# Two output tiles of a weight chunk take turns, matmul by matmul

## The chip, the cores and the metric

The kernel runs on one core of a Trainium2 chip. The metric is the device time of one execution in microseconds; smaller is better. Times before are three runs; the profile is of one execution.

## What is computed

A transformer-like stack on a sequence of 512 tokens with a model width of 1024, all in float32: twice (feed-forward, a mixer of three attention-like branches, feed-forward), then a second mixer and a feed-forward, then a last norm. Most of the arithmetic is products of an activation (1024 or 2816 by 512, held transposed) with a weight matrix. Cut to what matters:

```python
def swiglu_ffn(x, norm, w_gate, w_up, w_down):
    h = rms_norm(x, norm)
    return (jax.nn.silu(h @ w_gate) * (h @ w_up)) @ w_down

    for l in range(DEPTH):
        x = x + 0.5 * swiglu_ffn(x, ffn1_norm[l], ffn1_w_gate[l], ffn1_w_up[l], ffn1_w_down[l])
        h = rms_norm(x, mix_norm[l])
        aq, ak, av, bq, bk, bv, cq, ck, cv, cg, gates = jnp.split(h @ w_in[l], split_points, axis=-1)
...
        x = x + merged.astype(x.dtype) @ w_out[l]
        x = x + 0.5 * swiglu_ffn(x, ffn2_norm[l], ffn2_w_gate[l], ffn2_w_up[l], ffn2_w_down[l])
```

## The kernel before

Every product with a weight matrix goes through `linear` (or, where the output is wanted with tokens on the partitions, through `linear_tok`, which the change does not touch). The float32 operands are split into a high and a low part: a weight chunk `k_raw` becomes `k_wh` (ScalarE copies it, rounded) and `k_wl` (VectorE subtracts), an activation tile `k_x` becomes a high tile (`k_xh`, `k_uh`, the even tiles of `k_G`) and a low one (`k_xl`, `k_ul`, the odd ones). A product is then three matmuls into one PSUM bank: high weight by high activation, high weight by low activation, low weight by high activation. In the profile these are the rows `bank<-k_xh,k_wh`, `bank<-k_xl,k_wh` and `bank<-k_xh,k_wl`.

`linear` walks over its output columns in groups of 256, which are two output tiles (`nt` is 2) with a PSUM bank each. The four banks of `self.LIN` (bank0 to bank3) serve it, so one pair is drained while the next is filled. For a group it walks over the rows of the weights in chunks of up to four tiles of 128 (`kc`), 512 KB each. Within a chunk, before, the loop over the two tiles `m` is outside and the loop over the up to four `k` inside: 12 matmuls into one bank, then 12 into the other. There are 12,168 such matmuls (12,144 of them in pairs of tiles); `linear_tok` has 672 more.

At the first chunks and at each chunk's start, `chunk` emits a weight split two chunks ahead, into one of three buffers (`SPLIT`), which takes its place in ScalarE's and VectorE's queues behind what is already there. Each queue is played strictly in the order in which this Python program appended to it.

Other work is written as generators in `self.bg` (norms, attention, drains of finished banks). `quantum` lets every generator take one step. What a step appends to PE's queue stands between two matmuls of the linear; I call such a piece a burst. Some generators hold a step back until the program's own estimate of PE's clock has passed the estimated end of what they wait for (`ready`). Before, `quantum` is called after every third matmul of a linear.

When a group is finished, its two drains are appended to `self.bg`, each with the token `done[m]` of the last matmul into its bank. The first matmul into a bank waits for the drain that freed it (`fr`).

Two places matter below. In the first feed-forward, the first groups use `k_uh` and `k_ul`, which are the input times its gain but not yet divided by its root mean square; the drains `dgate` and `dup` multiply by it (`self.R`, `k_r`) afterwards. It comes out of `norm_r`: a matmul `bank<-k_acc,k_const` over the summed squares, three ScalarE steps, three VectorE steps. And at the end of a mixer, `merged` (`k_m0mrg`) is split into `k_xh` and `k_xl` before the `w_out` linear can begin.

Of the kernel before, what the change touches and what calls it, by code (L numbers as in the profile page):

```python
# [11 lines left out]
P = 128  # L12
# [112 lines left out]
class Program:  # L125
# [228 lines left out]
    def linear(self, name, l, r0, kts, c0, ncols, act, drain, rate=1, kc=KC):  # L354

        t = 0
        for g in range(0, ncols, 256):
            nt = min(256, ncols - g) // P
            banks = [self.take(self.LIN) for _ in range(nt)]
            done = [None] * nt  # L360
            k0 = 0
            while k0 < kts:
                kt = min(kc if nt == 2 else 2 * kc, kts - k0)
                i, wh, wl, th, tl = self.chunk(name, l, r0 + k0 * P, kt, c0 + g, nt * P)
                for m in range(nt):
                    b, fr = banks[m]
                    for k in range(kt):
                        xh, xl, t1, t2 = act(k0 + k)
                        lh, ll = wh[:, k, m * P:(m + 1) * P], wl[:, k, m * P:(m + 1) * P]
                        first, end = k0 + k == 0, k0 + k == kts - 1  # L370
                        self.mm(fr + [th, t1], b, lh, xh, first, False)
                        self.mm([t2], b, lh, xl, False, False)
                        last = k == kt - 1
                        tok = self.mm([tl], b, ll, xh, False, end, inc=last)
                        if not last:
                            self.quantum(rate)
                    done[m] = tok
                    if m < nt - 1:
                        self.quantum(rate)
                self.release(i, done[-1])  # L380
                k0 += kt
                if k0 < kts:
                    self.quantum(rate)
            for m in range(nt):
                self.bg.append(drain(t + m, banks[m][0], done[m]))
            t += nt
            self.quantum(rate)
# [1264 lines left out]
```

How the kernel before makes its waits and increments, by code:

```python
    def play(self, eng):  # L102
        for kind, a, b in self.items:
            if kind == 0:
                eng.wait_ge(a, b)
            elif kind == 1:
                a(eng)
            else:
                a(eng).then_inc(b, 1)
# [117 lines left out]
    def load(self, out, src, w=()):  # L227
        self.nld += 1
        self.G.wait(w)
        sem = self.ldsem
        self.G.run(lambda e: e.dma_start(out, src).then_inc(sem, 16))
# [1 line left out]
    def load_t(self, i, out, src, w):  # L234
        self.ntl[i] += 1
        self.G.wait(w)
        sem = self.tsem[i]
        self.G.run(lambda e: e.dma_start(out, src).then_inc(sem, 16))
        return (f"t{i}", sem, 16 * self.ntl[i])
# [29 lines left out]
    def _dma(self, i):  # L270
        name, l, r0, kt, c0, n = self.plan[i]
        w = self.d[name]
        src = w[l, r0:r0 + kt * P, c0:c0 + n].rearrange("(k p) n -> p k n", p=P)
        dst = self.RW[i % RAW][:, 0:kt * n].rearrange("p (k n) -> p k n", k=kt)
        self.S.wait(self.raws.pop(i - RAW, []))
        sem = self.rawsem[i % RAW]
        self.S.run(lambda e: e.dma_start(dst, src).then_inc(sem, 16))
# [762 lines left out]
    def mixer2(self, nextg):  # L1040
# [26 lines left out]
                    src = self.d[nm][0, 2 * m + j]  # L1067
                    sem = self.wbsem
                    self.G.run(lambda e, dst=dst, src=src, sem=sem: e.dma_start(dst, src).then_inc(sem, 16))
        twb = ("wb", self.wbsem, 16 * 16)
```

## Time and profile before

| | us |
|---|---|
| median of 3 runs | 3420.56 |
| lowest, highest | 3419.51, 3420.67 |
| span of the profiled execution | 3420.8 |

The profile gives no other time for its own execution than its span, which is 0.2 us above the median of the three runs and 0.1 us above the slowest of them. PE is TensorE's matmuls, PEld its weight loads, DVE is VectorE, ACT is ScalarE. A matmul's row shows its start and a length of about 0.39 us, but the next one starts about 0.23 us later: they overlap. So distances between starts are what counts.

### The profile page before, as it was taken

Reading aid. Unit: us, or ns where it says so; the run is one execution under the profiler, and the core shown is the slowest. Engines: PE = TensorE matmul, PEld = TensorE weight load, DVE = VectorE, ACT = ScalarE, POOL = GpSimd, SP = SyncE. Lnnn points to the kernel's source line nnn. Section 1 sums busy time; section 2 is a strip of 40 time slices with the busy share of each in tenths; the row PEclk is TensorE's granted clock in tenths of the full one; section 3 lists DMA queues with packets and bytes.
Section 4 is the critical chain, followed back from the end, with each engine's and each line's share of the span. In section 5 each row is a group of like instructions: output and inputs, shape, how many; then the busy total and the mean of one; then the engine's idle time right before and its main releaser. Section 6 shows DMA issues by size and latency. Waiting matters only on the chain.

```text
span 3420.8 us, 35895 instructions
## 1 busy us (share of the span) xinstructions
PE 3363.2 (98%) x14282; PEld 2601.9 (76%) x14282; DVE 1746.2 (51%) x2858; ACT 1255.8 (37%) x1891; POOL 28.6 (1%) x57
## 2 busy tenths in 40 slices
PE   7999999999999999999999999999999998999998
PEld 6888866577788888888876666888888756878886
DVE  6333687635463335433487744455334557884333
ACT  4222446424243233322355533334223346343232
POOL 0000000000000000000000000000000100000000
PEclk9999999999999999999999999999999999999999
DMA  4333321222223332333321222323332533323332
GB/s 140 102 95 90 94 73 53 71 80 77 93 87 105 93 95 90 105 99 95 96 85 51 71 64 78 92 92 94 99 93 87 109 61 50 84 80 99 98 91 70
DMA packets 282071, 297.66 MB, mean 87 GB/s; under 512 B 9776, under 2 KB 270256, under 8 KB 281904
## 3 DMA queue, kind: packets, MB, share of 16 engines
q1 hardware_dynamic: 277408, 283.15, 28.9%
q0 software_dynamic: 3536, 10.55, 1.0%
q8 instruction: 112, 1.84, 0.2%
q10 hardware_dynamic: 960, 1.67, 0.1%
q14 instruction: 55, 0.45, 0.0%
HBM read 293.24 MB, written 2.10 MB: 86 GB/s over the span
## 4 chain that ended last, share of the span: by engine, by line
PE 91%; DVE 5%; ACT 2%; issue 1%; DMA 0%; DVEq 0%; SPq 0%; ACTq 0%
PE bank L218 90%; ACT k_sc L214 1%; PE bank L224 1%; DVE k_wl L170 1%; DVE k_sc L180 1%; DVE k_sc L196 0%; DMA k_raw<-in_ffn_w_gate 0%; ACT L208 0%; DVE k_sc L170 0%; DVE k_x L180 0%; ACT k_wh L214 0%; DVE k_xc L180 0%; DVE k_xl L170 0%; DVE k_cv L180 0%; DVE k_ul L170 0%
## 5 line engine op out<-in xcount | busy, mean ns | idle before, releaser
L170 DVE TENSOR_TENSOR k_wl<-k_raw,k_wh 128x1024 fp32r<-128x1024 f32 x545 | 654.6, 1204 | 1178.6 <-ACT k_wh L214 1178.4
L218 PE MATMUL bank<-k_xh,k_wh 128*128 128x512 f32 x2376 | 960.7, 404 | 5.0 <-ACT k_wh L214 3.3
L218 PE MATMUL bank<-k_xh,k_wl 128*128 128x512 f32 x2376 | 928.9, 391 | 4.7 <-DVE k_wl L170 4.7
L218 PE MATMUL bank<-k_xl,k_wh 128*128 128x512 f32 x2376 | 928.4, 391 | 1.7 <-DVE k_xl L170 1.7
L214 ACT ACTIVATE k_wh<-k_raw 128x1024 fp32r<-128x1024 f32 x545 | 563.9, 1039 | 990.3 <-PE bank L218 721.6
L218 PEld LDWEIGHTS bank<-k_xh,k_wh 128*128 128x128 f32 x2376 | 447.2, 188 | 164.1 <-issue 67.9
L218 PEld LDWEIGHTS bank<-k_xh,k_wl 128*128 128x128 f32 x2376 | 447.5, 188 | 100.3 <-DVE k_wl L170 5.5
L218 PEld LDWEIGHTS bank<-k_xl,k_wh 128*128 128x128 f32 x2376 | 447.8, 188 | 96.7 <-issue 8.1
L218 PE MATMUL bank<-k_uh,k_wh 128*128 128x512 f32 x512 | 206.2, 403 | 18.6 <-ACT k_uh L214 18.5
L218 PE MATMUL bank<-k_Ga,k_wh 128*128 128x512 f32 x704 | 218.2, 391 | 0.0
L218 PE MATMUL bank<-k_Gb,k_wh 128*128 128x512 f32 x704 | 218.2, 391 | 0.0
L218 PE MATMUL bank<-k_uh,k_wl 128*128 128x512 f32 x512 | 202.5, 396 | 3.8 <-DVE k_wl L170 3.8
L218 PE MATMUL bank<-k_ul,k_wh 128*128 128x512 f32 x512 | 201.7, 394 | 0.2 <-DVE k_ul L170 0.2
L214 ACT ACTIVATE k_sc<-bank 128x512 f32<-128x512 f32 x160 | 94.6, 596 | 243.8 <-PE bank L218 243.8
L218 PEld LDWEIGHTS bank<-k_Ga,k_wh 128*128 128x128 f32 x704 | 132.2, 188 | 28.0
L218 PEld LDWEIGHTS bank<-k_Gb,k_wh 128*128 128x128 f32 x704 | 132.2, 188 | 28.0
L218 PE MATMUL bank<-k_Ga,k_wl 128*128 128x512 f32 x352 | 138.0, 392 | 0.0
L218 PE MATMUL bank<-k_Gb,k_wl 128*128 128x512 f32 x352 | 138.0, 392 | 0.0
L218 PEld LDWEIGHTS bank<-k_uh,k_wh 128*128 128x128 f32 x512 | 96.8, 189 | 42.4 <-ACT k_uh L214 19.0
L218 PEld LDWEIGHTS bank<-k_ul,k_wh 128*128 128x128 f32 x512 | 97.0, 189 | 25.5 <-issue 2.9
L218 PEld LDWEIGHTS bank<-k_uh,k_wl 128*128 128x128 f32 x512 | 97.0, 189 | 24.8 <-DVE k_wl L170 4.5
L213 ACT ACTIVATE k_sc<-k_sc,k_sm 128x128 f32<-128x128 f32 (+3 forms) x160 | 88.8, 555 | 70.9 <-DVE k_sm L175 70.8
(278 smaller groups left out, 3687.9 us busy)
## 6 DMA issues: line engine op xcount, KB each, us to landing
k_raw<-in_w_in SPq DMA_DIRECT2D x153, 512.0 KB, 3.7
k_raw<-in_ffn_w_gate SPq DMA_DIRECT2D x88, 512.0 KB, 3.8
k_raw<-in_ffn_w_up SPq DMA_DIRECT2D x88, 512.0 KB, 3.8
k_raw<-in_ffn_w_down SPq DMA_DIRECT2D x80, 512.0 KB, 3.4
k_raw<-in_w_out SPq DMA_DIRECT2D x28, 512.0 KB, 3.4
k_raw<-in_w_gate SPq DMA_DIRECT2D x22, 512.0 KB, 3.8
k_raw<-in_w_up SPq DMA_DIRECT2D x22, 512.0 KB, 3.8
k_raw<-in_w_down SPq DMA_DIRECT2D x20, 512.0 KB, 3.4
```

Source lines behind the costliest of these rows:

```text
L170: return q.op(lambda e: e.tensor_tensor(out, a, b, op), cost(out))
L180: return self.V.op(lambda e: e.scalar_tensor_tensor(out=out, in0=a, scalar=s, in1=b, op0=op0, op1=op1), cost(out))
L213: return self.A.op(lambda e: e.activation(out, a, f, bias=bias, scale=scale, accum_out=accum), c + 0.1)
L214: return self.A.op(lambda e: e.activation(out, a, f, bias=bias, scale=scale), c)
L218: fn = lambda e: e.matmul(out, l, r, start=start, stop=stop, skip_group_check=True)
L224: fn = lambda e: e.transpose(out, a, ident)
```

## The change

The loop over `k` is now outside, and inside it the two tiles take turns at each of the three products: high by high for tile 0 and tile 1, high by low for both, low by high for both. The sums into each bank are the same ones in the same order.

```diff
@@ -362,21 +362,19 @@
                 i, wh, wl, th, tl = self.chunk(name, l, r0 + k0 * P, kt, c0 + g, nt * P)
-                for m in range(nt):
-                    b, fr = banks[m]
-                    for k in range(kt):
-                        xh, xl, t1, t2 = act(k0 + k)
-                        lh, ll = wh[:, k, m * P:(m + 1) * P], wl[:, k, m * P:(m + 1) * P]
-                        first, end = k0 + k == 0, k0 + k == kts - 1
-                        self.mm(fr + [th, t1], b, lh, xh, first, False)
-                        self.mm([t2], b, lh, xl, False, False)
-                        last = k == kt - 1
-                        tok = self.mm([tl], b, ll, xh, False, end, inc=last)
-                        if not last:
+                for k in range(kt):
+                    xh, xl, t1, t2 = act(k0 + k)
+                    first, end, last = k0 + k == 0, k0 + k == kts - 1, k == kt - 1
+                    cols = [slice(m * P, (m + 1) * P) for m in range(nt)]
+                    for m in range(nt):
+                        b, fr = banks[m]
+                        self.mm(fr + [th, t1], b, wh[:, k, cols[m]], xh, first, False)
+                    for m in range(nt):
+                        self.mm([t2], banks[m][0], wh[:, k, cols[m]], xl, False, False)
+                    for m in range(nt):
+                        done[m] = self.mm([tl], banks[m][0], wl[:, k, cols[m]], xh, False, end, inc=last)
+                        if not last or m < nt - 1:
                             self.quantum(rate)
-                    done[m] = tok
-                    if m < nt - 1:
-                        self.quantum(rate)
                 self.release(i, done[-1])
```

Three places of the built programs show it. In each row, the tile left of the arrow is written and those right of it are read; trailing numbers are buffer numbers.

**The first chunk, PE.** Before, here from the tenth matmul of the kernel, the twelfth is the last into bank0 and the thirteenth the first into bank1:

```order
L218 MATMUL bank0<-k_uh_124,k_wh_113 128x512
L218 MATMUL bank0<-k_ul_125,k_wh_113 128x512
L218 MATMUL bank0<-k_uh_124,k_wl_114 128x512
L218 MATMUL bank1<-k_uh_124,k_wh_113 128x512
L218 MATMUL bank1<-k_ul_125,k_wh_113 128x512
L218 MATMUL bank1<-k_uh_124,k_wl_114 128x512
```

Now, from the first matmul of the kernel:

```order
L218 MATMUL bank0<-k_uh_124,k_wh_113 128x512
L218 MATMUL bank1<-k_uh_124,k_wh_113 128x512
L218 MATMUL bank0<-k_ul_125,k_wh_113 128x512
L218 MATMUL bank1<-k_ul_125,k_wh_113 128x512
L218 MATMUL bank0<-k_uh_124,k_wl_114 128x512
L218 MATMUL bank1<-k_uh_124,k_wl_114 128x512
```

Neighbours write different banks and read the same activation tile; the calls of `quantum` stand behind the fifth and sixth of six matmuls in place of behind the third and sixth.

**The first norm, PE.** The matmul over the summed squares (`k_acc_120`) of the first feed-forward stands behind 66 matmuls of linears before; the rows end at the 69th:

```order
L218 MATMUL bank3<-k_uh_124,k_wh_113 128x512
L218 MATMUL bank3<-k_ul_125,k_wh_113 128x512
L218 MATMUL bank3<-k_uh_124,k_wl_114 128x512
L218 MATMUL bank4<-k_acc_120,k_const_115 128x512
L218 MATMUL bank3<-k_uh_124,k_wh_113 128x512
L218 MATMUL bank3<-k_ul_125,k_wh_113 128x512
L218 MATMUL bank3<-k_uh_124,k_wl_114 128x512
```

Now it stands behind 71, one before the last of the third chunk (the rows end at the 73rd):

```order
L218 MATMUL bank3<-k_uh_124,k_wh_113 128x512
L218 MATMUL bank2<-k_ul_125,k_wh_113 128x512
L218 MATMUL bank3<-k_ul_125,k_wh_113 128x512
L218 MATMUL bank2<-k_uh_124,k_wl_114 128x512
L218 MATMUL bank4<-k_acc_120,k_const_115 128x512
L218 MATMUL bank3<-k_uh_124,k_wl_114 128x512
L218 MATMUL bank2<-k_uh_124,k_wh_113 128x512
```

It has moved by five matmuls, from the middle of the third chunk to its end, where the next weight split is emitted.

**The same norm, ACT and DVE.** ACT, from the table load ahead of it; before, `k_sc<-bank,k_eps` and the two `k_r` are the norm's steps, and the next weight split (`k_wh`) comes four rows behind them, outside this piece:

```order
L214 ACTIVATE k_wh<-k_raw 128x1024
L214 ACTIVATE k_sc<-bank,k_eps 128x512
L214 ACTIVATE k_r<-k_sc 128x512
L214 ACTIVATE k_r<-k_r 128x512
L214 ACTIVATE k_xh<-k_sc 128x512
L214 ACT_TABLE_LOAD
```

Now:

```order
L214 ACTIVATE k_wh<-k_raw 128x1024
L214 ACTIVATE k_sc<-bank,k_eps 128x512
L214 ACTIVATE k_r<-k_sc 128x512
L214 ACTIVATE k_r<-k_r 128x512
L214 ACTIVATE k_wh<-k_raw 128x1024
L214 ACTIVATE k_xh<-k_sc 128x512
L214 ACT_TABLE_LOAD
```

A `k_wh` stands directly behind the norm's two `k_r`. DVE, before: the norm's three steps are the second to fourth row, and the `x2` row behind `k_x` is the two drains of the first group:

```order
L170 TENSOR_TENSOR k_wl<-k_raw,k_wh 128x1024
L180 SCALAR_TENSOR_TENSOR k_sc<-k_sc,k_r 128x512
L170 TENSOR_TENSOR k_sc<-k_sc,k_r 128x512
L180 SCALAR_TENSOR_TENSOR k_r<-k_sc,k_r 128x512
L180 SCALAR_TENSOR_TENSOR k_sc<-k_x,k_vec,k_r 128x512
L170 TENSOR_TENSOR k_sc<-bank,k_r 128x512 x2
L170 TENSOR_TENSOR k_wl<-k_raw,k_wh 128x1024
```

Now:

```order
L170 TENSOR_TENSOR k_wl<-k_raw,k_wh 128x1024 x2
L180 SCALAR_TENSOR_TENSOR k_sc<-k_sc,k_r 128x512
L170 TENSOR_TENSOR k_sc<-k_sc,k_r 128x512
L180 SCALAR_TENSOR_TENSOR k_r<-k_sc,k_r 128x512
L180 SCALAR_TENSOR_TENSOR k_sc<-k_x,k_vec,k_r 128x512
L170 TENSOR_TENSOR k_sc<-bank,k_r 128x512 x2
L170 TENSOR_TENSOR k_sc<-bank,k_sc 128x512
```

The second weight split (`x2` in the first row) stands ahead of the norm's three steps; before, it stood behind the two drains.

## Rows read from the trace of the kernel before

**Rows 1.** The page, whole span: busy time by engine; the chain that ended last.

```profile
PE 3363.2 (98%) x14282; PEld 2601.9 (76%) x14282; DVE 1746.2 (51%) x2858; ACT 1255.8 (37%) x1891; POOL 28.6 (1%) x57
...
PE bank L218 90%; ACT k_sc L214 1%; PE bank L224 1%; DVE k_wl L170 1%; DVE k_sc L180 1%; DVE k_sc L196 0%; DMA k_raw<-in_ffn_w_gate 0%; ACT L208 0%; DVE k_sc L170 0%; DVE k_x L180 0%; ACT k_wh L214 0%; DVE k_xc L180 0%; DVE k_xl L170 0%; DV
```

**Rows 2.** Timeline, PE, first stage (start us, length us, what).

```profile
22.82 0.39 PE L218 MATMUL bank<-k_uh,k_wl 128*128 128x512 f32 x1
23.05 0.39 PE L218 MATMUL bank<-k_uh,k_wh 128*128 128x512 f32 x1
23.28 0.39 PE L218 MATMUL bank<-k_ul,k_wh 128*128 128x512 f32 x1
```

**Rows 3.** Timeline, PE, in `linear_tok`: two ends of 30 matmuls.

```profile
745.80 0.39 PE L218 MATMUL bank<-k_wh,k_xh 128*128 128x512 f32 x1
...
752.38 0.39 PE L218 MATMUL bank<-k_wl,k_xh 128*128 128x512 f32 x1
```

**Rows 4.** Timeline, PE, `linear` at 1000 us: two ends of 52 matmuls.

```profile
1000.15 0.39 PE L218 MATMUL bank<-k_ul,k_wh 128*128 128x512 f32 x1
...
1011.82 0.39 PE L218 MATMUL bank<-k_ul,k_wh 128*128 128x512 f32 x1
```

**Rows 5.** Timeline, PE, an attention matmul and the two behind it.

```profile
468.64 0.49 PE L218 MATMUL bank<-k_m0qkva 64*128 64x128 f32 x2
469.05 0.50 PE L218 MATMUL bank<-k_wh,k_xh 128*128 128x512 f32 x1
469.39 0.40 PE L218 MATMUL bank<-k_wh,k_xl 128*128 128x512 f32 x1
```

**Rows 6.** Timeline, 35 to 44 us, PE, ACT and DVE.

```profile
35.41 1.02 PE L218 MATMUL bank<-k_acc,k_const 128*128 128x512 f32 x2
...
43.15 0.39 PE L218 MATMUL bank<-k_uh,k_wh 128*128 128x512 f32 x1
...
36.86 0.67 ACT L214 ACTIVATE k_sc<-bank,k_eps 128x512 f32<-128x512 f32 x1
...
38.23 0.63 ACT L214 ACTIVATE k_r<-k_r 128x512 f32<-128x512 f32 x1
...
37.52 1.23 DVE L170 TENSOR_TENSOR k_wl<-k_raw,k_wh 128x1024 fp32r<-128x1024 f32 x1 [1.13 <-ACT k_wh L214]
38.89 0.69 DVE L180 SCALAR_TENSOR_TENSOR k_sc<-k_sc,k_r 128x512 f32<-128x512 f32 x1 [0.15 <-ACT k_r L214]
...
41.07 0.75 DVE L180 SCALAR_TENSOR_TENSOR k_sc<-k_x,k_vec,k_r 128x512 f32<-128x512 f32 x1
41.74 1.28 DVE L170 TENSOR_TENSOR k_sc<-bank,k_r 128x512 f32<-128x512 f32 x2
```

**Rows 7.** Timeline, start of the first `w_out`, PE and DVE.

```profile
936.40 0.40 PE L218 MATMUL bank<-k_m0yc,k_wl 128*128 128x512 f32 x1
937.60 0.47 PE L218 MATMUL bank<-k_xh,k_wh 128*128 128x512 f32 x1 [0.81 <-ACT k_xh L214]
938.90 0.50 PE L218 MATMUL bank<-k_xl,k_wh 128*128 128x512 f32 x1 [0.82 <-DVE k_xl L170]
...
936.83 0.69 DVE L180 SCALAR_TENSOR_TENSOR k_sc<-k_sc,bank 128x512 f32<-128x512 f32 x1 [1.29 <-PE bank L218]
...
938.16 2.49 DVE L170 TENSOR_TENSOR k_xl<-k_m0mrg,k_xh 128x512 fp32r<-128x512 f32 x4
```

**Rows 8.** Stretches (us, busy (x count) of PE, PEld, DVE, ACT, POOL, PEclk, DMA, GB/s).

```profile
940.00:944.00 4.00, 4.00 (x12) 3.16 (x11) 4.00 (x7) 2.05 (x4) 0.00 (x0) 0.57 0.00 0
944.00:948.00 4.00, 4.00 (x19) 3.30 (x18) 0.90 (x2) 1.06 (x1) 0.00 (x0) 1.00 0.39 131
```

**Rows 9.** Waits of PE: us in total, times, longest.

```profile
PE bank L218 <- DVE k_wl L170: 8.5, 3, 4.1
...
PE bank L218 <- DVE k_pt L188: 2.8, 1, 2.8
```

**Rows 10.** Timeline, DVE, the last linear's drains.

```profile
3400.99 0.69 DVE L180 SCALAR_TENSOR_TENSOR k_x<-bank,k_x 128x512 f32<-128x512 f32 x1 [8.04 <-PE bank L218]
```

## The prediction

> **What bounds the kernel now.** I read the page first. PE is busy for 98% of the span and the chain that ended last runs through `bank L218` for 90% [rows 1]: the reader is to see that nothing but the pace of the matmuls, and the places where PE waits, can move the time. The loads are as many as the matmuls (14,282 each) and are covered. Then the timeline of PE gives the pace. In `linear`, 51 distances between starts take 11.67 us, 0.229 us each [rows 4]. The list of PE's waits names only few and short ones in the middle [rows 9]. So the 12,168 matmuls of `linear` at 0.229 are some 2,786 us of the 3420.8.
>
> **The bank change.** Now neighbours write different banks all along. The kernel before has such neighbours at times, so their price can be read off. The twelfth matmul of the kernel (22.82) is the last into bank0, the next (23.05) the first into bank1: 0.23 us, and the one behind it, in the same bank as its forerunner, again comes after 0.23 [rows 2]. In `linear_tok` the bank changes after every sixth matmul, twice as often as in `linear`, and 29 distances with four or five changes among them take 6.58 us, 0.227 each [rows 3]; 51 distances of `linear` with four or five changes have 0.229 [rows 4]. More changes do not go with a slower pace, so a change costs nothing. Nor do rows 2 show a gain at one. With some 11,100 changes added (12,144 less about 1,000 that were there), I price the change of bank at 0. Two distances rounded to 0.01 leave room for 0.01 either way; a cost of that size is excluded by `linear_tok`, a gain is the rival that is far from the rest, and stands there with its chance.
>
> The Trainium skill (TensorE: Matmul & The Clock Gate, "Back-to-back issue gap") gives for 512 columns an isolated gap of about 216 ns. This trace shows 229. Were the difference of 13 ns due to the bank and given back, it would be some 158 us, about 3262.
>
> As a mechanism of this kernel it would be a PSUM bank that is still being written when the next matmul wants it; the rival further down prices that from rows.
>
> Two more things of the new order cost nothing by rows: that neighbours read the same moving tile (in `linear_tok` the first and second of three do, at 0.227, [rows 3]), and that weights now alternate (there is a load to each matmul already, [rows 1]).
>
> **What the change moves.** Five places, each worked out with 0.229 a matmul.
>
> First, the first group's drains, in the first feed-forward. The norm's matmul moves back by five, 1.14 us, from 35.41 to 36.55; it takes 1.02, so ScalarE begins about 37.7. Its three steps took from 36.86 to 38.86, 2.0 us [rows 6], so they end at 39.7. Before, VectorE then began the norm's last steps at 38.89 and the first drain of the banks at 41.74, 2.85 later [rows 6]. Now a weight split stands between: 1.04 on ScalarE and about 1.2 on VectorE (the row at 37.52 has 1.23). That puts the norm's steps at 41.9, the first drain at 44.75, its end (0.64, half of 1.28) at 45.4, the second one's at 46.0. PE wants bank0 at 43.15 [rows 6]; before, the drain was done 0.8 earlier. So it stands 2.25 us, and since its second matmul now wants bank1 at once and not twelve matmuls later, another 0.4: **2.65**. If ScalarE's first step comes as late behind the matmul as before (1.45) it is 3.0; if the split's two steps overlap others, 1.5. Behind the waiting matmul stands all of PE's queue, so the whole of it counts.
>
> Second, the clock. After PE had been idle for two stretches of 0.8 us close to each other at 937 to 939 us [rows 7], the granted clock was 0.57 over 940 to 944, 12 matmuls in place of 4.00 / 0.229 = 17.5, and 1.00 behind it [rows 8]: 5.5 x 0.229 = **1.3**, the level of 1.2 GHz for most of that stretch. A stall of 2.65 is at least as long. Either 0 or 1.3; I take 1.3.
>
> Third, the two starts of `w_out`. `merged` is needed whole. Before, tile 0 of the last pair was done 12 matmuls ahead of tile 1, and VectorE had worked it off; it took up tile 1 at 936.83 and the low splits at 938.16 [rows 7]. Now both are done within one matmul, VectorE begins at 936.6 and has four steps of 0.69 in place of two, so the splits begin at 939.3, 1.15 later. The low product is now the third matmul and not the second, which covers 0.23. PE loses 0.9 each time, twice: **1.8**. Both ends: 0, if the split were still covered, and 2 x 1.4 = 2.8, four steps less two without any cover.
>
> Fourth, the end. The last chunk has two `k`, so tile 0 led by six matmuls and VectorE's drain began at 3400.99 [rows 10], with a strictly serial chain behind it up to the output. It leads by one now: 5 x 0.229 = **1.1** later. Nothing covers it.
>
> Fifth, the gain. The low weights are wanted by the fifth matmul of a chunk in place of the third. PE waited for them three times, 8.5 us in all [rows 9], and each wait becomes 2 x 0.229 shorter: **-1.4**.
>
> Everything else that the later `done[0]` delays (drains of other groups) is read by nobody for a whole group of 24 or 48 matmuls, 5.5 or 11 us, against 1.4 us of drains; I cost it at nothing. If that cover went, PE would wait at most those 1.4 us at a group.
>
> **The bursts.** Steps of the background work now come two close together and then none for five matmuls. Counted in the built programs, 202 bursts with a matmul of 64 rows or columns stay 202, and all bursts go from 315 to 307. A burst with such a matmul has an exit price: from 468.64 over 469.05 to 469.39 are 0.75 us for 128 columns in four passes (0.21) and one matmul (0.23), so 0.3 more [rows 5]. Their number stays, so 0. New is that 81 matmuls stand alone between two bursts, which occurs nowhere before. The nearest row is the distance behind a burst, 0.34 in place of 0.23 [rows 5]: a lone matmul might pay it once more or be spared it, 81 x 0.11 = 9 us either way. I take 0, because the switches between the two kinds of matmul are the same in number.
>
> In the second mixer the bursts move by up to 77 matmuls, so PE's wait of 2.8 us for `k_pt` [rows 9] can go, or another come; 0, between -2.8 and +2.8.
>
> **Sum.** 2.65 + 1.3 + 1.8 + 1.1 - 1.4 = 5.45. On the profiled execution's 3420.8 that is 3426.25; its span is 0.2 above the median, so I predict 3426, 0.16% slower than 3420.56. What a measurement of this kernel can tell from no change is about 0.2%, 6.8 us (3427.4). I forecast no difference that can be told, on the slow side.
>
> **The rivals.**
> - *Slower: the lone matmuls.* If each of the 81 pays the 0.11 again, 9 us come on top: 3435. For it: nothing in the trace shows that one matmul is enough to get back the overlap. Against it: the number of switches is the same. It decides from 0.02 us each on, with the sum above. 0.20.
> - *The first stall does not come* (the split is done earlier than the queue suggests, or the planner's distance suffices): 2.65 + 1.3 go, 3422. Against it: the queues are strictly in order, and the drains had 0.8 us left before. 0.10, of which 0.03 with a lucky second mixer and spared bursts below 3413.7.
> - *Faster: the bank was a limit after all.* 12,144 x (0.229 - 0.213) = 194 us, 3226. For it: 512 columns at 2.4 GHz, one a cycle, would be 0.213. Against it: rows 2 to 4. 0.04.
> - *Slower by the clock.* The Trainium skill (same page, "A second HAM failure mode: psum-queue depth-cycling") tells of a kernel that cycled through banks and idled so briefly and often that the clock kept falling. As a mechanism here: every bank change would have to leave a gap, and the clock fall as in rows 8; then a tenth of the linears at half pace would be 12,168 x 0.1 x 0.2 = 243 us, 3664. Against it: bank changes leave no gap in rows 2 and 4. 0.02.
> - My forecast has the rest, 0.64, and its own range is 3419 to 3432. Its terms can add up to more than 6.8 us (stall 3.0, `w_out` 2.8, second mixer +2.8), so I count 0.16 of it as slower.
>
> **How the numbers follow.** Faster: 0.04 + 0.03 = 0.07. Slower: 0.16 + 0.20 + 0.02 = 0.38. Same: 0.48 + 0.07 = 0.55. The range leaves out the two far cases (0.06) and something at each side: below, the unknown costs of the second mixer and of spared bursts, above, the lone matmuls with the forecast's upper terms. 3418 to 3438.
>
> **What would show it.** In the profile after: PE's distances in a long run of `linear` still 0.229 (right) or nearer 0.215 (the bank was a limit). A wait of PE of 2 to 3 us for VectorE's `k_sc` around 43 us, with a stretch of granted clock near 0.5 behind it. The low product of both `w_out` about 1 us later behind the end of the branch. The last chain about 1 us longer. PE's waits for `k_wl` three, some 7 us. Behind lone matmuls between bursts, a distance of 0.34 or more twice would show the first rival. The prediction is wrong if PE's pace changes at all: 0.001 us a matmul is 12 us.

## The result, and the profile after

The changed kernel takes 3436.81 us (median of 4 runs, 3433.58 to 3438.15), against 3420.61 of the kernel before in the same session (4 runs, 3419.51 to 3421.85): a ratio of 1.0046, 95% interval 1.0034 to 1.0058. It is slower by 0.5%, over twice the 0.2% (6.8 us) that the prediction gave as the least that can be told from no change. The prediction was 3426, within a range of 3418 to 3438, with most of its chance on no difference that can be told.

The profiled execution is the fastest of the four: 3433.58 us, span 3431.8. In the runs listed the time is 1.8 to 2.0 us above the span. So the profiled execution of the kernel before (span 3420.8) was one of some 3422.7 us, about 2 us above its median, and not 0.2 as the prediction had it. The two traces are therefore 11.0 us apart and the medians 16.2. What the traces can explain is the 11.0.

The page after, the lines that answer to [rows 1]:

```profile
PE 3361.6 (98%) x14282; PEld 2606.0 (76%) x14282; DVE 1738.0 (51%) x2853; ACT 1253.3 (37%) x1898; POOL 28.6 (1%) x57
...
PE bank L218 91%; PE bank L224 1%; ACT k_sc L214 1%; DVE k_wl L170 1%; DVE k_sc L180 1%; DVE k_sc L196 0%; DMA k_raw<-in_ffn_w_gate 0%; DVE k_sc L170 0%; ACT k_wh L214 0%; ACT L208 0%; DVE k_x L180 0%; DVE k_xc L180 0%; DVE k_cv L180 0%; DV
```

PE is as busy as before, to 1.6 us. The pace has not changed either. PE in `linear` at 1000 us, where each row is now two matmuls into two banks; the two ends of 27 rows:

```profile
1004.24 0.62 PE L218 MATMUL bank<-k_uh,k_wl 128*128 128x512 f32 x2
...
1016.14 0.62 PE L218 MATMUL bank<-k_ul,k_wh 128*128 128x512 f32 x2
```

From the first to the last are 26 rows, 52 distances, in 11.90 us: 0.229 each, as in [rows 4], now with a change of bank at every one.

From the waits of PE over the whole kernel, those at the end and at the two starts of `w_out` (us in total, times, longest):

```profile
PE bank L218 <- DVE k_acc L170: 3.9, 1, 3.9
...
PE bank L218 <- DVE k_xl L170: 3.4, 2, 1.7
```

And the start of the kernel, which answers to [rows 6]: PE, then ACT, then DVE.

```profile
36.53 1.02 PE L218 MATMUL bank<-k_acc,k_const 128*128 128x512 f32 x2
...
45.41 0.50 PE L218 MATMUL bank<-k_uh,k_wh 128*128 128x512 f32 x1 [2.13 <-DVE k_sc L170]
...
38.98 0.63 ACT L214 ACTIVATE k_r<-k_r 128x512 f32<-128x512 f32 x1
39.51 1.04 ACT L214 ACTIVATE k_wh<-k_raw 128x1024 fp32r<-128x1024 f32 x1
...
40.69 1.23 DVE L170 TENSOR_TENSOR k_wl<-k_raw,k_wh 128x1024 fp32r<-128x1024 f32 x1 [1.97 <-ACT k_wh L214]
41.83 0.68 DVE L180 SCALAR_TENSOR_TENSOR k_sc<-k_sc,k_r 128x512 f32<-128x512 f32 x1
...
44.67 1.28 DVE L170 TENSOR_TENSOR k_sc<-bank,k_r 128x512 f32<-128x512 f32 x2
```

The norm's matmul stands at 36.53, the split `k_wh` directly behind the norm's two `k_r`, the norm's steps on VectorE begin at 41.83 (before: 38.89), the drain at 44.67 and PE goes on at 45.41, after 2.13 us of idling. The prediction had these at 36.55, 41.9, 44.75 and 45.4.

Where the time comes in shows when the same matmul is looked up in both traces. The n-th matmul of the linears (`linear` and `linear_tok` together, 12,840) starts at:

| n | before | after | later by |
|---|---|---|---|
| 66 | 35.19 | 35.16 | 0.0 |
| 97 | 43.15 | 45.41 | 2.3 |
| 240 | 75.88 | 80.20 | 4.3 |
| 3312 (last ahead of the first `w_out`) | 936.40 | 940.49 | 4.1 |
| 8592 | 2308.61 | 2312.57 | 4.0 |
| 10176 (second mixer begins) | 2670.25 | 2674.21 | 4.0 |
| 10608 | 2833.85 | 2830.41 | -3.4 |
| 10800 | 2890.89 | 2897.34 | 6.4 |
| 11350 (its end) | 3062.71 | 3073.53 | 10.8 |
| 12840 (last) | 3401.94 | 3412.76 | 10.8 |

Three stretches matter: 4.3 us in the first feed-forward, 6.9 in the second mixer, and 1.1 at the end, of which the trace shows 0.2 (below). Between 80 and 2670 us little is left on balance (0.4 us gained), although bursts with lone matmuls between them lie all along it.

The waits of PE in the second mixer grow by the same 6.9. Of the kernel before, beside the 8.5 for `k_wl` and the 2.8 for `k_pt` in [rows 9], which all lie here:

```profile
...
PE bank L218 <- ACT k_wh L214: 3.3, 1, 3.3
...
PE bank L218 <- ACT k_ycat L214: 0.8, 2, 0.6
PE bank L224 <- DVE k_xdt L170: 0.8, 1, 0.8
PE bank L218 <- DVE k_ycat L170: 0.4, 2, 0.2
PE bank L218 <- DVE k_sc L170: 0.4, 1, 0.4
PE bank L218 <- DVE k_xc L180: 0.4, 1, 0.4
PE bank L218 <- DVE k_ul L170: 0.2, 1, 0.2
```

And of the changed one, all of them:

```profile
PE bank L218 <- ACT k_wh L214: 11.9, 2, 9.4
PE bank L218 <- DVE k_wl L170: 3.6, 2, 3.5
PE bank L224 <- DVE k_xdt L170: 3.3, 1, 3.3
PE bank L224 <- DVE k_sc L175: 2.2, 1, 2.2
PE bank L218 <- DVE k_x L180: 1.4, 1, 1.4
PE bank L224 <- DVE k_pt L188: 1.1, 1, 1.1
PE bank L218 <- DVE k_x L170: 0.6, 1, 0.6
PE bank L218 <- DVE k_sc L170: 0.4, 1, 0.4
```

They add up to 17.6 us before and 24.5 after. It is not one wait that grew: `k_wl` went from 8.5 to 3.6, `k_wh` from 3.3 to 11.9, and `k_xdt`, `k_sc` and `k_x` are new or longer.

### The profile page after: what moved, and what is told of

The parts are those of the page before. It is cut to its first block, busy times and chain, and to the rows that moved or that the text cites. A ratio compares the mean times of both kernels' runs of the same rounds, so it can differ in the third digit from the quotient of the medians.

```text
span 3431.8 us, 35884 instructions
## 1 busy us (share of the span) xinstructions
PE 3361.6 (98%) x14282; PEld 2606.0 (76%) x14282; DVE 1738.0 (51%) x2853; ACT 1253.3 (37%) x1898; POOL 28.6 (1%) x57
## 4 chain that ended last, share of the span: by engine, by line
PE 92%; DVE 4%; ACT 2%; issue 1%; DMA 0%; DVEq 0%; SPq 0%; ACTq 0%
PE bank L218 91%; PE bank L224 1%; ACT k_sc L214 1%; DVE k_wl L170 1%; DVE k_sc L180 1%; DVE k_sc L196 0%; DMA k_raw<-in_ffn_w_gate 0%; DVE k_sc L170 0%; ACT k_wh L214 0%; ACT L208 0%; DVE k_x L180 0%; DVE k_xc L180 0%; DVE k_cv L180 0%; DVE k_xc L170 0%; ACT k_ycat L214 0%
## 5 line engine op out<-in xcount | busy, mean ns | idle before, releaser
L218 PE MATMUL bank<-k_xh,k_wl 128*128 128x512 f32 x2376 | 774.7, 399 | 0.2 <-DVE k_wl L170 0.2
L218 PE MATMUL bank<-k_xh,k_wh 128*128 128x512 f32 x2376 | 746.7, 395 | 13.5 <-ACT k_wh L214 11.9
L218 PE MATMUL bank<-k_xl,k_wh 128*128 128x512 f32 x2376 | 735.9, 391 | 3.4 <-DVE k_xl L170 3.4
L218 PE MATMUL bank<-k_Gb,k_wh 128*128 128x512 f32 x704 | 190.3, 392 | 0.0
L218 PE MATMUL bank<-k_Ga,k_wh 128*128 128x512 f32 x704 | 190.3, 392 | 0.0
L218 PE MATMUL bank<-k_uh,k_wh 128*128 128x512 f32 x512 | 164.2, 401 | 22.2 <-ACT k_uh L214 18.5
L218 PE MATMUL bank<-k_uh,k_wl 128*128 128x512 f32 x512 | 164.0, 400 | 3.5 <-DVE k_wl L170 3.5
L218 PE MATMUL bank<-k_ul,k_wh 128*128 128x512 f32 x512 | 160.3, 395 | 0.0
L170 DVE TENSOR_TENSOR k_sc<-bank,k_sc 128x512 f32<-128x512 f32 x110 | 75.6, 687 | 130.2 <-PE bank L218 128.7
L180 DVE SCALAR_TENSOR_TENSOR k_x<-bank,k_x 128x512 f32<-128x512 f32 x104 | 69.7, 686 | 87.1 <-PE bank L218 86.3
```

Of the source, the lines that this page charges most:

```text
L170: return q.op(lambda e: e.tensor_tensor(out, a, b, op), cost(out))
L180: return self.V.op(lambda e: e.scalar_tensor_tensor(out=out, in0=a, scalar=s, in1=b, op0=op0, op1=op1), cost(out))
L218: fn = lambda e: e.matmul(out, l, r, start=start, stop=stop, skip_group_check=True)
```

## The experiments

The experiments were run in three later sessions, in which the kernel before had medians of 3421.11 (experiments 1 to 4), 3420.79 (5 to 8) and 3420.64 us (9 to 12). The ratios are to these. The changed kernel was not run again, so a difference to its 3436.81 us can be off by some 0.5 us.

**1. The calls of `quantum` where they were, the turns kept.** The bank turns stay as in the change; the background's steps are spread over six matmuls as before.

```diff
                     for m in range(nt):
                         self.mm([t2], banks[m][0], wh[:, k, cols[m]], xl, False, False)
+                        if nt == 2 and m == 0:
+                            self.quantum(rate)
                     for m in range(nt):
                         done[m] = self.mm([tl], banks[m][0], wl[:, k, cols[m]], xh, False, end, inc=last)
-                        if not last or m < nt - 1:
+                        if m == nt - 1 and not last:
                             self.quantum(rate)
```

> The tiles take turns as in the change, but the background work gets its steps after every third matmul again, as before. Theory (the change of bank costs nothing; of the 11 us that the profile of the changed kernel is longer, some 7 arise in the second mixer, where the background work stands at other places): the second mixer's bursts are back at their old places, so those 7 us go and what is left is the later first norm with its stall (4), the two starts of w_out (1.4) and the end (1.1), less the shorter waits for low weights (0.9): 3420.6 + 5 to 6 = 3426. Rival (the alternation itself costs, by banks or by lone matmuls): all neighbours still change banks, so it stays at 3434 to 3438.

Measured: 3429.88 us (10 runs, 3427.74 to 3433.94), ratio 1.0026 (1.0017 to 1.0035). It lies between the theory and the rival. About 7 us of the 16 are due to where the calls stand; 9 are left with the turns alone. The theory had 5 to 6, since it took all of the second mixer's 6.9 us to be the calls': PE's waits there are 20.3 us in this kernel, in place of 17.6 before and 24.5 after, 3.3 of them for `k_xdt`. The norm's stall (1.7), the waits at `w_out` and the one at the end are still there.

**2. The old order of matmuls, the calls clumped.** The mirror image: 12 matmuls into one bank, then 12 into the other, but `quantum` behind the fifth and sixth of six.

Against the kernel before:

```diff
-                        tok = self.mm([tl], b, ll, xh, False, end, inc=last)
-                        if not last:
+                        for j, (w, l_, r_) in enumerate(((fr + [th, t1], lh, xh), ([t2], lh, xl), ([tl], ll, xh))):
+                            tok = self.mm(w, b, l_, r_, first and j == 0, end and j == 2, inc=last and j == 2)
+                            n += 1
+                            if n % 6 == 5 or (n % 6 == 0 and n < 3 * nt * kt):
+                                self.quantum(rate)
...
-                    if m < nt - 1:
-                        self.quantum(rate)
```

> The order of the matmuls is that of before (12 into one bank, 12 into the other), but the background work gets its steps after the fifth and sixth of every six matmuls, as in the change; 75 matmuls stand alone between bursts. Theory (the places of the background work do it): the second mixer loses about as much as with the change, 5 to 12 us; the first norm stands behind 65 matmuls, so no stall there, and w_out and the end are as before: 3426 to 3432. Rival (banks or the alternation): 3420.6, within 2 us.

Measured: 3433.04 us (5 runs, 3431.2 to 3434.49), ratio 1.0035 (1.0022 to 1.0049), 1 us above the theory's range. A kernel in which the banks do not take turns loses 12 us. In its waits:

```profile
PE bank L218 <- ACT k_wh L214: 12.2, 3, 9.1
PE bank L218 <- DVE k_wl L170: 4.9, 3, 3.8
...
PE bank L218 <- ACT k_m0qkvb L214: 2.7, 1, 2.7
```

`k_wh` and `k_wl` are close to those of the changed kernel. Its own are a wait of 2.7 us for `k_m0qkvb` in the first mixer and one like it in the other: 5.4 of the 12 us are a cost that the changed kernel does not have. The bank as the cause is out, and so is the idea that the loss needs both tiles to end together.

**3. The old loop in the two linears of the second mixer.**

```diff
+                if name in ("w_in_2", "w_out_2"):
...
+                    for m in range(nt):
+                        b, fr = banks[m]
+                        for k in range(kt):
...
+                else:
```

> The changed kernel, but the linears of the second mixer (in and out) use the loop of before. Theory: the 7 us of the second mixer in the profile (and up to 12 in the slower runs) go and with them the spread of the runs: 3426, with runs within 1 us. Rival (cost spread over all alternating matmuls): 984 of 12,168 matmuls go back, so under 10 per cent of the 16 us: 3435.

Measured: 3427.39 us (11 runs, 3426.41 to 3429.75), ratio 1.0019 (1.0011 to 1.0028); 9.4 less than the changed kernel, and near the theory's 3426, though its runs still spread over 3.3 us, which the theory had not. Between the two profiled executions, each the fastest of its kernel, it is 7.2. The waits in the second mixer are those of before again (`k_wl` 8.6, `k_wh` 3.3, `k_pt` 2.8).

**4. The old loop in the first five chunks.**

```diff
+                if self.ci <= 4:
...
+                    for m in range(nt):
+                        b, fr = banks[m]
+                        for k in range(kt):
...
+                else:
```

> The changed kernel, but the first groups (first five chunks) use the loop of before, so that the norm's matmul stands behind 66 matmuls again and the weight split behind the drains. Theory (the stall of 2.3 us at the third group and the lower clock behind it, 2.0): 4.2 us less than the changed kernel, 3432.6, and no wait of PE near 43 us. Rival (the stall comes from the drains being bunched, not from the norm's place): the stall stays, 3436.8.

Measured: 3431.68 us (7 runs, 3428.32 to 3432.18), ratio 1.0029 (1.0018 to 1.004); 5.1 less. PE has no wait near 43 us in this kernel. The stretch of 36 to 48 us, first of the changed kernel, then of this one (us, busy (x count) of PE, PEld, DVE, ACT, POOL, PEclk, DMA, GB/s):

```profile
36.00:48.00 12.00, 9.77 (x37) 7.09 (x36) 7.31 (x11) 6.91 (x9) 0.00 (x0) 0.92 0.31 90
```

```profile
36.00:48.00 12.00, 12.00 (x52) 9.53 (x51) 7.34 (x11) 7.00 (x10) 0.00 (x0) 1.00 0.15 46
```

37 matmuls recorded in place of 52, and the granted clock 0.92 in place of 1.00.

**5. One split ahead of the recurrence's chain.** The largest new wait is `k_wh`, 9.43 us at 2907.15. ScalarE and VectorE there, in the changed kernel:

```profile
2900.87 1.28 ACT L214 ACT_TABLE_LOAD   x1
2905.53 0.63 ACT L214 ACTIVATE k_sc<-k_sc 128x512 f32<-128x512 f32 x1 [3.38 <-DVE k_sc L180]
2906.06 1.04 ACT L214 ACTIVATE k_wh<-k_raw 128x1024 fp32r<-128x1024 f32 x1
...
2901.41 3.35 DVE L196 RECIPROCAL k_sc<-k_sc 128x512 f32<-128x512 f32 x1
2904.80 0.69 DVE L180 SCALAR_TENSOR_TENSOR k_sc<-k_sc 128x512 f32<-128x512 f32 x1
2907.23 1.23 DVE L170 TENSOR_TENSOR k_wl<-k_raw,k_wh 128x1024 fp32r<-128x1024 f32 x1 [1.74 <-ACT k_wh L214]
```

The split stands behind a square root, which waits for the 3.35 us reciprocal of the recurrence. This kernel lets the last recurrence hold back its VectorE steps, so that on both engines the split stands ahead of it; TensorE's order is untouched.

```diff
+                for _ in range(3 if m == 3 else 0):
+                    yield
                 t = self.ts([tt1, ta], r, h_, 1.0, None, ALU.add)
                 t = self.rcp([t], r, r)
```

> The changed kernel; in the second mixer the last of four recurrences holds back its three VectorE steps around the reciprocal by three steps of the background. TensorE's order is untouched; on ScalarE the weight split k_wh stands ahead of the square root, on VectorE k_wl ahead of the 3.35 us reciprocal, and nothing else moves. Theory (the time lost in the second mixer is a split that stands behind this chain): ScalarE is free for k_wh at 2900.9, so TensorE goes on at 2902 in place of 2907.15; the wait of 9.4 us becomes some 4 to 5, 5 us less: 3431.5. Rival (the loss of the second mixer is spread over its bursts, and the wait only shows where it is booked): the next chunk waits for what this one no longer does, within 1.5 us of the changed kernel, 3436.

Measured: 3435.88 us (5 runs, 3435.82 to 3437.68), ratio 1.0043 (1.0031 to 1.0056). The theory fell. PE at that place:

```profile
2901.72 0.73 PE L218 MATMUL bank<-k_xh,k_wh 128*128 128x512 f32 x2 [4.13 <-ACT k_wh L214]
...
2903.08 1.22 PE L218 MATMUL bank<-k_xh,k_wl 128*128 128x512 f32 x2 [0.16 <-DVE k_wl L170]
...
2915.00 1.19 PE L218 MATMUL bank<-k_xh,k_wh 128*128 128x512 f32 x2 [5.56 <-ACT k_wh L214]
```

4.13 + 0.16 + 5.56 = 9.85 in place of 9.43. The next split has to stand behind the chain instead, and PE waits there. As far as this run shows, the sum of the waits is set by how long ScalarE and VectorE need for what stands in their queues, not by the place of one split in it. No run shortens that work, so this is as near as the runs come.

**6. The old loop in three places at once**: the first five chunks, the second mixer's linears, the last chunk of every group.

```diff
+                if name in ("w_in_2", "w_out_2") or self.ci <= 4 or k0 + kt == kts:
...
+                    for m in range(nt):
+                        b, fr = banks[m]
+                        for k in range(kt):
...
+                else:
```

> The changed kernel with the old loop over matmuls in three places: the first five chunks, the two linears of the second mixer, and the last chunk of every group. About three quarters of all matmuls of linear still alternate between banks. Theory (all that the change costs lies at these places, the turns of the banks cost nothing): stage 0 gives back 3.9 to 4, the second mixer 6.9, the drain at the end 1.1, the starts of w_out some 1: 3421 to 3424. Rival (part of the cost is spread over the alternating matmuls or the lone ones): of the 16 us some 4 or more stay, 3425 and above.

Measured: 3417.44 us (11 runs, 3416.43 to 3418.8), ratio 0.9989 (0.998 to 0.9998). Nothing of the 16 us is left, although about half of the neighbouring matmuls of `linear` in its built program (6,269 pairs of 11,906; 11,896 of 11,912 in the changed kernel, 961 of 11,904 before) still write different banks. It is even 3.4 us below the kernel before, which its interval still tells from equal, though it is less than 0.2%. Between the start and the second mixer its trace gains 0.9 and 0.8 us in the two first mixers, and 1.8 us at each `w_out`, most of which is the clock (below). Why the mixers gain was not tried.

**7. The kernel before, its tiles 64 bytes higher.** In the trace before, matmuls that read `k_xh` and `k_xl` went at 0.2274 us on the mean (7,230 distances) and those that read from the region behind `self.phase` (`k_uh`, `k_ul`, the tiles of feed-forwards and mixers) at 0.2291 (4,899 distances). The region starts at 127,936 bytes in each partition, 64 short of a multiple of 1024; the lower tiles start at 128 past one.

```diff
-        self.phase = (self.off + 63) // 64 * 64
+        self.phase = (self.off + 127) // 128 * 128
```

> The kernel before with one number changed: the region in which the activation tiles of mixers and feed-forwards lie starts at a multiple of 128 bytes in each partition in place of a multiple of 64 (64 bytes higher). The order of all engines is the same. In the kernel before, long runs of linear that read from this region go at 0.229 us a matmul and runs that read from the lower part of the memory at 0.2274. Theory (the start address of the moving tile makes the 1.7 ns): some 4,900 matmuls get 1.7 ns shorter, 8 to 9 us less, 3412. Rival (the region or the kind of tile does it, not the address): 3421, within 1.5.

Measured: 3438.01 us (5 runs, 3436.03 to 3439.5), ratio 1.0047 (1.0034 to 1.0061). Both expectations missed: the address matters, and the multiple of 1024 is slower, not faster. PE at 1000 us, the two ends of 51 matmuls:

```profile
1001.76 0.39 PE L218 MATMUL bank<-k_uh,k_wl 128*128 128x512 f32 x1
...
1013.43 0.39 PE L218 MATMUL bank<-k_ul,k_wh 128*128 128x512 f32 x1
```

50 distances in 11.67 us, 0.2334 each, at a granted clock of 1.00 throughout.

**8. The kernel before, with its split ahead of the chain.** As experiment 5, by two steps; only VectorE's order changes, `k_wl` ahead of the reciprocal.

```diff
+                for _ in range(2 if m == 3 else 0):
+                    yield
                 t = self.ts([tt1, ta], r, h_, 1.0, None, ALU.add)
```

> The kernel before; in the second mixer the last of four recurrences holds back its three VectorE steps around the reciprocal by two steps of the background. The orders of TensorE and ScalarE are untouched; on VectorE k_wl stands ahead of the 3.35 us reciprocal. Theory (a split behind this chain costs what it waits): the wait for k_wl of 4.1 us at 2895 to 2899 goes to about 0.5 and the half pace of the clock behind it may go too (up to 1.4 us): 3416 to 3417.5. Rival (the chain that is now later makes TensorE wait elsewhere by the same): 3420 to 3421.

Measured: 3424.54 us (11 runs, 3423.48 to 3426.71), ratio 1.001 (1.0001 to 1.0019), so 3.7 slower. PE at that place:

```profile
2892.19 0.50 PE L218 MATMUL bank<-k_xh,k_wh 128*128 128x512 f32 x1 [3.30 <-ACT k_wh L214]
...
2893.55 0.71 PE L218 MATMUL bank<-k_xh,k_wl 128*128 128x512 f32 x1 [0.63 <-DVE k_wl L170]
...
2905.47 0.76 PE L218 MATMUL bank<-k_xh,k_wh 128*128 128x512 f32 x1 [5.04 <-ACT k_wh L214]
```

3.30 + 0.63 + 5.04 = 8.97, where the kernel before waits 3.33 + 4.10 + 0.56 = 7.99. The wait moved on again and grew, since the chain now starts later. The rival, with a loss on top.

**9 and 10. The kernel before, its region 128 and 192 bytes higher** (64 and 128 past a multiple of 1024).

```diff
-        self.phase = (self.off + 63) // 64 * 64
+        self.phase = (self.off + 63) // 64 * 64 + 128
```

> The kernel before with the region of the mixers' and feed-forwards' tiles 128 bytes higher in each partition: it starts at 64 past a multiple of 1024 bytes, where before it started 64 short of one (0.2291 us a matmul that reads there), and in the run with the region 64 bytes higher exactly at one (0.2331). Theory (only the place within 128 bytes counts): as before, 3421. Rival (the place within 1024 bytes counts, and the worst is at its multiple): between the 0.2274 of the tiles in the lower part and 0.2331, so 3412.5 to 3438.

> The kernel before with the same region 192 bytes higher: it starts at 128 past a multiple of 1024 bytes, where the tiles of the lower part stand as well, whose matmuls take 0.2274 us. Theory (the place within 1024 bytes counts): some 4,900 matmuls get from 0.2291 to 0.2274, 8.3 us less, 3412.5. Rival (only the place within 128 bytes counts): as with the region 64 bytes higher, 3438.

Measured: 3438.75 us (5 runs, 3438.57 to 3441.66), ratio 1.0054 (1.0042 to 1.0067), for 128 bytes; 3412.15 us (7 runs, 3410.29 to 3413.19), ratio 0.9972 (0.9962 to 0.9983), for 192. The second one's PE at 1000 us, again the ends of 51 matmuls:

```profile
994.63 0.39 PE L218 MATMUL bank<-k_ul,k_wh 128*128 128x512 f32 x1
...
1005.97 0.39 PE L218 MATMUL bank<-k_uh,k_wh 128*128 128x512 f32 x1
```

11.34 us, 0.2268 each. So it is not the place within 128 bytes: 64 short of a multiple of 1024 and 64 past it are the same place by that, and went at 0.229 and 0.233. The place within 1024 fits all runs; a longer period than that was not tried.

**11. As experiment 6, with turns in the second mixer too, but the calls evenly spaced there.**

```diff
-                if name in ("w_in_2", "w_out_2") or self.ci <= 4 or k0 + kt == kts:
+                if name in ("w_in_2", "w_out_2"):
...
+                            if nt == 2 and m == 0:
+                                self.quantum(rate)
...
+                elif self.ci <= 4 or k0 + kt == kts:
```

> As the kernel with the old loop in three places (3417.4), but in the linears of the second mixer the banks take turns too, with the calls of quantum evenly behind every third matmul as before the change. Theory (the loss in the second mixer comes from calls that stand two close together and so move the bursts, not from the turns): the bursts stand as before up to a matmul or two, at most 1.7 us more, 3417.4 to 3419.1. Rival (the turns do it, because both tiles of a pair end together): 6.9 us more, 3424.

Measured: 3420.84 us (11 runs, 3419.81 to 3421.69), ratio 1.0 (0.9991 to 1.0008): 3.4 more than experiment 6, half way between that kernel and the rival's 3424. Its waits in the second mixer:

```profile
PE bank L218 <- DVE k_wl L170: 7.0, 2, 3.6
PE bank L218 <- ACT k_wh L214: 3.7, 2, 3.3
PE bank L224 <- DVE k_xdt L170: 3.3, 1, 3.3
PE bank L218 <- DVE k_pt L188: 2.8, 1, 2.8
PE bank L218 <- DVE k_x L180: 2.3, 2, 1.6
```

They add up to 21.0, which is 3.4 above the 17.6 of the kernel before. 2.5 of it is that the wait for `k_xdt` is longer, the same 3.3 as in the changed kernel: the first of the two convolution drains (`k_cv`, 3.1 us each on VectorE) begins 4.7 us before PE wants `k_xdt` (2933.88 and 2938.60), in place of 7.2 in the kernel before (2937.18 and 2944.42), since both wait for the end of the pair.

**12. Experiments 6 and 10 together.**

```diff
-        self.phase = (self.off + 63) // 64 * 64
+        self.phase = (self.off + 63) // 64 * 64 + 192
...
+                if name in ("w_in_2", "w_out_2") or self.ci <= 4 or k0 + kt == kts:
```

> The kernel with the old loop in three places (3417.4), with the region of tiles 192 bytes higher. If the address brings 8.3 us in the kernel before, it brings them here too: 3409, faster than both kernels. If the run with the same move in the kernel before is slower, this one is slower by as much: 3434.

Measured: 3406.39 us (5 runs, 3405.77 to 3406.79), ratio 0.9957 (0.9943 to 0.9971). It beats both kernels. 3.4 of its 14.3 us are experiment 6's, 8.5 experiment 10's; 2.4 are more than their sum.

## Why the prediction was right and where it was wrong

**The number: inside the range, in part by luck.** 3437 lies 1.2 us inside the stated 3418 to 3438, on the side that was forecast. But it is outside the forecast's own 3419 to 3432, and "no difference that can be told" did not come true: 16.2 us are more than 6.8. The stated range went up to 3438 to leave room for the lone matmuls, which cost nothing. The terms at the start, at `w_out` and at the end came close to what was forecast; the term for the second mixer failed.

**The bank change, priced at 0: right.** The pace is 0.229 before and after, and experiment 2 loses 12 us without it while experiment 6 keeps it at half of the distances and loses nothing. "The bank was a limit after all" is out. Of the pace 2.3 ns go with an address (experiment 10), and 0.2268 is the least that a run here shows. The Trainium skill (TensorE: Matmul & The Clock Gate, "Back-to-back issue gap") has an isolated gap of about 216 ns; that 13 ns lie between it and this kernel is not the bank's doing.

**The first drains, 2.65: right.** PE waited 2.13 us for bank0, and its next matmul, now into bank1, began 0.60 us behind that one in place of 0.23 (46.01, 45.41). By that matmul, the 98th, the changed kernel is 2.63 us later than the kernel before, and the four steps named above stand within 0.1 us of their forecasts. Experiment 4 takes the wait away.

**The clock, 1.3: right in kind, 0.4 too small.** From the 98th to the 240th matmul another 1.70 us are lost. The granted clock was 0.50 from 46.05 to 49.47 us, the level of 1.2 GHz, with 8 matmuls 0.427 us apart in place of 0.229, which is 1.6 us; that is why the stretch of 36 to 48 us in experiment 4 has 0.92. The prediction took 12 matmuls from [rows 8]; that count includes those that only reach into the stretch, and 10 begin in it, which would have given 1.7. Together with the stall it is 4.3 in place of 3.95.

**The starts of `w_out`, 1.8: right, and hidden in this trace.** The wait for `k_xl` went from 0.8 to 1.7 us each time, 1.7 in all. But behind these waits the clock falls or does not, from one start and one trace to the next. The stretches that follow the two starts in the changed kernel:

```profile
943.60:947.60 4.00, 3.52 (x9) 2.82 (x10) 4.00 (x8) 2.55 (x5) 0.00 (x0) 0.57 0.00 0
2269.00:2273.00 4.00, 3.41 (x15) 2.83 (x16) 4.00 (x7) 2.66 (x5) 0.00 (x0) 1.00 0.00 0
```

0.57 behind the first, the level of 1.2 GHz for most of it, and 1.00 behind the second. In the profiled execution of before it fell at both, in those of experiments 6 and 8 at neither. One such fall is 1.6 us, as above. So the two starts cost nothing on balance between these two traces, and 1.7 by the waits.

**The end, 1.1: right.** PE's wait for `k_acc` went from 2.8 to 3.9, which is 1.1. The norm's last matmul then ran at full clock and not at half as before (1.12 us in place of 2.07), which gave 0.95 back in this execution; in eight of the twelve other kernels here it took 2.1 (in the rest 1.1 to 1.8).

**The gain at `k_wl`, -1.4: came at one place of three.** The first of the three waits, ahead of the chain at 2683, went from 3.8 to 3.5. The other two lie in the second mixer's chain, where `k_wh` took them over: `k_wl` fell by 4.9 in all and `k_wh` rose by 8.6. There this term and the next are one.

**The second mixer, "0, between -2.8 and +2.8": the step that failed.** The wait for `k_pt` did go, to 1.1 from 2.8, as it might. What I had not seen is that a whole stretch of this mixer is not bound by PE's pace but by serial work on ScalarE and VectorE: four recurrences, with a reciprocal of 3.35 us on VectorE and table loads of 1.28 us between the functions on ScalarE in each, and the splits behind them in the same queues. In the trace before, the chain that ended last spends the stretch of 2834.75 to 2907.39 us on these two engines and none of it on PE; 7.4 of its 8.5 + 3.3 us of waits for `k_wl` and `k_wh` stand within 9 us there, at 2891 to 2900.

Each recurrence is fed by a burst of PE (two matmuls that read `k_xc`). In the built programs the first two of these stand behind 10,590 and 10,617 matmuls of the linears before, and behind 10,607 and 10,631 in the changed kernel; experiment 2 has the places of the changed kernel, experiments 1, 3 and 11 those of before. The first two of the four reciprocals, before and then in the changed kernel:

```profile
2834.75 3.35 DVE L196 RECIPROCAL k_sc<-k_sc 128x512 f32<-128x512 f32 x1
...
2849.86 3.35 DVE L196 RECIPROCAL k_sc<-k_sc 128x512 f32<-128x512 f32 x1
```

```profile
2838.05 3.35 DVE L196 RECIPROCAL k_sc<-k_sc 128x512 f32<-128x512 f32 x1
...
2858.18 3.35 DVE L196 RECIPROCAL k_sc<-k_sc 128x512 f32<-128x512 f32 x1
```

They are 15.1 us apart before and 20.1 after. From the first to the fourth it is 59.4 us before, 63.4 in the changed kernel, 63.1 in experiment 2, and 59.4 or 59.5 in experiments 1, 3, 6 and 11. So the clumped calls, and not the turns, make this chain 4 us longer: they move the bursts that feed it. PE runs ahead meanwhile, 3.4 us at the 10,608th matmul, and then waits 9.4. The turns do the other part: pairs that end together start the convolutions late (experiment 11, 3.4 us). By the waits, the calls alone make 5.8 us (experiment 2: 23.4 in place of 17.6), the turns alone 3.4 (2.7 in experiment 1) and both together 6.9. Experiments 5 and 8 show that the place of one split in the queues does not matter much: 9.43 us became 9.85 and 7.99 became 8.97 when it was moved ahead.

**The bursts and lone matmuls, 0: right.** From the 240th matmul to the 8592nd the changed kernel gains 0.4 us, though 62 of the 81 lone matmuls lie there. PE's waits grew by 2.9 us in that stretch (1.7 for `k_xl`, 0.9 for `k_m0qkc` and `k_m1qkc`, 0.2 for `k_m0qkva` and `k_m1qkva`) and the clock fell once less (1.6), so 1.6 us were gained otherwise; from what stays open. The rival that priced them at 0.11 each would be 6.8 us there. Its time, 3435, was near, for another reason. The exit price of 0.3 was misread, without effect: the `x2` row of [rows 5] is two matmuls, at 468.64 and 468.85, so the 0.75 us hold two times 0.21 and one 0.23, and about 0.1 is left.

**The rest.** 16.2 us are measured and 11.0 seen between the traces: the profiled execution of the kernel before was slower than its median, that of the changed kernel the fastest of four. The runs' granted clock goes with it. The changed kernel's fastest run, the profiled one, has 0.994, the three others 0.993; of the kernel before, 17 runs of the last session, those up to 3421 us have 0.995 or 0.996, those above 3422.8 have 0.994. It is what one would expect if the clock fell at more of the waits in the slower runs, as it is seen to do at `w_out`. As an estimate: a fall of 3.4 us to 0.50 lowers the mean by 0.0005 and costs 1.6 us, so a mean that is 0.001 lower is two more falls, some 3 of the 5 us. The means are rounded to 0.001, so it can be much less or all of it. No trace of a slower run is kept, and these 5 us stay open.

The Trainium skill (same page, "A second HAM failure mode: psum-queue depth-cycling") stood beside the rival at 3664. This case's trace does not bear that rival out: the pace rows above have a change of bank at every matmul and the granted clock of 1004 to 1016 us is 1.00. The clock fell behind waits of PE: single ones of 0.8 us and more, and in the trace before also behind four of 0.2 to 0.6 us that follow each other from 3015 to 3018 us (granted 0.50 from 3018.84 to 3022.26).

## What to carry to other kernels

A share of 98% for an engine says nothing on the stretches where it waits for a chain. Look for waits that stand close together behind serial work of other engines, and for stretches of the last chain that the busy engine has no part in. Ask what feeds such a chain, and price every move of that at full size. Here, to move one item ahead in the queues of such a chain only moved the wait; to shorten the chain was not tried. And where a reordering of the main loop carries the calls of a background scheduler along, separate the two: here the turns alone cost 9 us, the place of the calls alone 12 (5 of them at waits that the two together do not have), and with the old loop at three sensitive places neither cost anything.

## What was not expected of the hardware

The start address of the tile that a matmul streams changes its pace. With the same program, at a granted clock of 1.00, matmuls of 512 columns that read a region starting 64 bytes short of a multiple of 1024 take 0.2288 to 0.2291 us, at the multiple 0.2334, at 64 past it 0.233 (the mean of 4,887 distances), at 128 past it 0.2268. About 5,000 of the linears' 12,168 matmuls read there (all but the 3 x 2376 of `k_xh` and `k_xl`). As measured, the region 64 bytes higher costs 17 us, 128 bytes 18, and 192 bytes gain 8.5; from the distances one would estimate some 20, 21 and 11. Why is open: the addresses of the weights stayed the same in all runs, so it can be the tile's own place or its distance from the weights' place, and no run here tells which.

At half the clock the address makes no difference. In experiment 7, whose region starts at the multiple, the granted clock is 0.50 from 2701.71 to 2705.12 us, and the eight matmuls that start from 2701.83 to 2704.81, which read `k_uh` and `k_ul`, are 0.427 us apart. The kernel before and the changed one have 0.427 at that level too, for tiles of both places. That is 512 columns at 1.2 GHz with nothing over, while 0.2268 to 0.2334 are all more than the 0.213 of 2.4 GHz. So what the address costs appears at the full clock alone.
